# Storing the activated feed-forward input by groups of four tokens, 35 and 37 lines apart, ahead of the down projection

## The chip, the core and the metric

The kernel runs on one core of a Trainium2 chip. The metric is the device time of one execution in microseconds (us), the median of several runs; lower is better.

## What is computed

Two transformer-like blocks run on 256 tokens of width 1024. The change touches only the last layer of the second block, a gated feed-forward network:

```python
D_MODEL = 1024
D_FF = 3 * D_MODEL
...
def second_block(x, mem, ...):
    ...
        x = x + merged @ w_out[l]

        h2 = rms_norm(x, norm_ffn[l])
        up = causal_dwconv(h2 @ w_up[l], ffn_conv_w[l], ffn_conv_b[l])
        gate_h, val_h = jnp.split(up, 2, axis=-1)
        x = x + (jax.nn.gelu(gate_h, approximate=True) * val_h) @ w_down[l]
    return rms_norm(x, final_norm)
```

The product of the gelu and `val_h` is the activated feed-forward input: 3072 features by 256 tokens. The last matrix product multiplies it by `w_down` (3072 x 1024).

## The kernel before

All activations are held transposed: features on the 128 partitions, tokens along the free dimension. A matrix of 1024 features is 8 tiles (`KD`) of 128 x 256; the activated input has 24 (`KF`).

**Precision.** Every product is made from two parts of each operand, a rounded high part and the rest as a low part, and three products: high weight by high input, high weight by low input, low weight by high input. Weights are streamed from HBM in tiles of 128 x 1024 (512 KB). SP issues the transfers into `raw` (two chunks of two tiles, v = 0 and 1). ACT rounds a tile into `w_hi[v]` (L1378), POOL, in some stages DVE, writes `w_lo[v] = raw - w_hi` (L466). TensorE waits for `hi_ready[v]` and `lo_ready[v]`, and gives `w_hi[v]` and `w_lo[v]` free by `hi_used[v]` and `tile_done[v]`.

**Token order in a matmul.** In nearly all products the 256 tokens of the moving operand are not read in their order in memory. `spread` (L432) turns them into four rounds: a round takes every fourth group of four tokens (16 bytes), so that successive groups lie 64 bytes apart; the output in PSUM is written by the same pattern, so each token's result still lands in its own place.

```python
def spread(tile):

    return tile.rearrange("p (j g c) -> p g j c", g=4, c=4)
```

**Up stage** (about 1376 to 1498 us of the span). TensorE makes chunk n of the up projection (48 matmuls, L679 and L698). For each chunk DVE scales the result (L2612), ACT makes the last tap of the convolution (L1861, twice), DVE the others (L2624), ACT the gelu (L1867), DVE the product with `val_h` into a PSUM tile `ffp` (L2639); then ACT rounds it into plane n of `f_hi` (L1872) and DVE writes `f_lo = ffp - f_hi` (L2644). ACT also rounds the two weight tiles of the next chunk in between. Planes n lie one behind the other, each 256 tokens in their order: `f_hi` and `f_lo` are [128, 24, 256].

**Down stage** (1498 to 1564.5 us). 12 chunks: four pairs of output tiles (`pr`) by three thirds of the features (`g`). For each chunk and each of its two weight tiles (v) come three times 8 matmuls of 128 x 128 by 128 x 256: `w_hi` by `f_hi`, `w_hi` by `f_lo`, `w_lo` by `f_hi` (L1282), 576 in all. They accumulate in half a PSUM bank each. Nothing else is on TensorE in this stage. The order is written out by hand in program order on each engine.

**Tail** (from 1564.5 us). The last output tile is added to the residual, and the final norm is made and stored.

`f_hi` and `f_lo` lie inside the large SBUF region `big`, between `m_lo` and `x_hi`, `x_lo`. `yout`, the output ahead of its store, is carved from `big` behind `f_lo` (at `AT_X`, over `x_hi`).

Of the kernel before, what the change touches and what calls it, by code (L numbers as in the profile page):

```python
# [30 lines left out]
F32R = mybir.dt.float32r  # L31
# [3 lines left out]
ALU = mybir.AluOpType  # L35
ACT = mybir.ActivationFunctionType
AX = mybir.AxisListType

P = 128
T = 256  # L40
TT = T // P
D = 1024
KD = D // P
# [6 lines left out]
GROUP = 8  # L50
GATE_PARTS = 2
GATE_SCALE = 2.0 ** 14


CONV_W = 31
# [20 lines left out]
KF = DFF // P  # L76
# [90 lines left out]
def build(nc, t):  # L167
    plan, order = plan_chunks()
    ctx = ExitStack()
    with ctx:  # L170
        def sb(name, shape, dt=F32):
            return ctx.enter_context(nc.sbuf_tensor(name, shape, dt))
# [13 lines left out]
        w_hi = [sb(f"w_hi{v}", [P, TILE], F32R) for v in range(2)]  # L186
        w_lo = [sb(f"w_lo{v}", [P, TILE], F32R) for v in range(2)]
# [28 lines left out]

        y_hi = sb("y_hi", [P, KD, T], F32R)
        y_lo = sb("y_lo", [P, KD, T], F32R)
        m_lo = sb("m_lo", [P, KD, T], F32R)
        f_hi = sb("f_hi", [P, KF, T], F32R)  # L220
        f_lo = sb("f_lo", [P, KF, T], F32R)
        x_hi = sb("x_hi", [P, KD, T], F32R)
        x_lo = sb("x_lo", [P, KD, T], F32R)
        AT_M, AT_X, AFTER_X = (n * KD * T for n in (2, 9, 11))

        def carver(base, start=0):
            at = [start]

            def carve(*shape, rows=P, dt=F32):
                n = math.prod(shape) // (2 if dt in (BF16, F16) else 1)  # L230
                v = base[0:rows, at[0]:at[0] + n]
                at[0] += n
                assert at[0] <= base.shape[1], (at[0], shape)
                if dt != F32:
                    v = v.bitcast(dt)[:, 0:math.prod(shape)]
                names = "abcd"[:len(shape)]
                if len(shape) == 1:
                    return v
                return v.rearrange(f"p ({' '.join(names)}) -> p {' '.join(names)}",
                                   **dict(zip(names, shape)))  # L240
            return carve
# [4 lines left out]
        carve = carver(big)  # L246
# [15 lines left out]
        carve = carver(big, AFTER_X)  # L262
# [10 lines left out]
        carve = carver(big, 64 * T)  # L273
# [14 lines left out]
        carve = carver(small)  # L288
# [7 lines left out]
            "p b n (g i o) -> p b n g i o", g=GROUP // 2, o=2)  # L296
        hot2 = carve(2, GROUP // 2 * P * 2, dt=F16).rearrange("p b (g i o) -> p b g i o", g=GROUP // 2, o=2)

        a_hi, a_lo = [act_parts[:, i:i + 4, :].rearrange("p (c v) t -> p c v t", c=2) for i in (0, 4)]
        memT = small[:, 0:KD * T].rearrange("p (k t) -> p k t", t=T)  # L300

        carve = carver(big, KD * T)
# [27 lines left out]
        carve = carver(big, AT_M)  # L330
# [4 lines left out]
        carve = carver(big, AT_M + 5 * KD * T)  # L335
# [3 lines left out]
        carve = carver(big, AT_M + 2 * KD * T)  # L339
        spare = carve(2, KD, C96)  # L340

        carve = carver(big, 3 * KD * T)
# [10 lines left out]
        carve = carver(small)  # L353
# [7 lines left out]
        carve = carver(big, KD * T)  # L361
        uc = carve(2, 2, T)
        ffg, ffp = [[aux[n + b][:, 0:T] for b in range(2)] for n in (0, 2)]
        carve = carver(big, AT_X)
        yout = carve(KD, T)
        DOWN_TILES = ((0, 2), (2, 4), (4, 6), (6, 7), (7, 8))
        OUT_TILES = ((0, 2), (2, 4), (4, 6), (6, 8))
        carve = carver(big, KD * T + 4 * T)
# [6 lines left out]
        hi_ready = [sem(f"hi_ready{v}") for v in range(2)]  # L375
        lo_ready = [sem(f"lo_ready{v}") for v in range(2)]
# [55 lines left out]
        def spread(tile):  # L432

            return tile.rearrange("p (j g c) -> p g j c", g=4, c=4)
# [222 lines left out]
        def _(pe):  # L657
# [205 lines left out]
            for k in range(2):  # L863
                mm = pe.matmul(aux[2][:, 0:T], ones[:, :], sq[:, k, :], start=(k == 0), stop=(k == 1))
# [42 lines left out]
            for k in range(KD // 2):  # L907
                mm = pe.matmul(aux[3][:, 0:T], ones[:, :], sq[:, k, :], start=(k == 0), stop=(k == KD // 2 - 1))
# [3 lines left out]
            for j in range(HEADS + 1):  # L912
                if j and j + 1 < HEADS:
                    scores(j + 1)
                if j:
                    turn_probs(j - 1)
                    name, i, v = beside_heads[j - 1]
# [20 lines left out]
            for g in range(TT * 4):  # L938
# [5 lines left out]
                for i in range(4):  # L944
                    v, at = divmod(h0 + i, HALVES // 2)
                    mm = pe.matmul(aux[g % 4][:, i * NK:(i + 1) * NK], qp[:, h0 + i, tt * P:(tt + 1) * P],  # L946
                                   raw[kc.raw][v][:, at * NK:(at + 1) * NK], start=True, stop=True)
# [14 lines left out]
            for n, src in enumerate((e1, e2, sc)):  # L962
                for tt in range(TT):
                    mm = pe.transpose(aux[n][:, tt * P:(tt + 1) * P],
                                      src[:, tt].rearrange("p h k -> p (h k)"), ident[:, :])
# [126 lines left out]
            for h in range(GH):  # L1092
                mm = pe.matmul(pair(aux[h // 2], GDK)[:, h % 2, :], wdec[:, h, :], dec, start=True, stop=True)
# [5 lines left out]
            for h in range(K96):  # L1099
                if h in MQ_TILES:  # L1100
                    n = MQ_TILES.index(h)
# [56 lines left out]
            for tt in range(TT):  # L1158
                for h in range(GH):
                    mm = pe.transpose(aux[tt][:, h * GDK:(h + 1) * GDK], ekd[:, h, tt * P:(tt + 1) * P],  # L1160
                                      ident[0:GDK, 0:GDK])
# [4 lines left out]
            for h in range(GH):  # L1166
                for n in range(NCH):
                    lo, cols = (n % 2) * GCHUNK, slice(n * GCHUNK, (n + 1) * GCHUNK)
                    at_col = (h * TT + n // 2) * GCHUNK
                    mm = pe.matmul(aux[2][lo:lo + GCHUNK, at_col:at_col + GCHUNK], emg[:, h, cols],  # L1170
                                   eg[:, h, cols], start=True, stop=True)
# [99 lines left out]
            for i, c in enumerate(plan["down"]):  # L1271
                pr, g = divmod(i, 3)
                if i == 0:
                    pe.wait_ge(ffn_act, KF - 1)
                pe.wait_ge(ffn_split, KD * (g + 1) if pr == 0 else KF)
                for v in range(2):
                    out = gemm[1][:, 0:T] if pr == 3 and v else pair(aux[pr])[:, v, :]
                    for w, x, ready in ((w_hi, f_hi, hi_ready), (w_hi, f_lo, hi_ready), (w_lo, f_hi, lo_ready)):
                        pe.wait_ge(ready[v], c.split + 1)
                        for k in range(KD):  # L1280

                            mm = pe.matmul(spread(out), w[v][:, k * P:(k + 1) * P], spread(x[:, g * KD + k, :]),  # L1282
                                           start=(g == k == 0 and (v == 0 or pr == 3) and w is w_hi and x is f_hi),
                                           stop=(g == 2 and w is w_lo and k == KD - 1), skip_group_check=True)
                        if x is f_lo:
                            mm.then_inc(hi_used[v], 1)
                    mm.then_inc(tile_done[v], 1)
                if pr == 1 and g == 1:
                    moved(pe, plan["up"])
# [18 lines left out]
        def _(act):  # L1308
# [560 lines left out]
            def ffn_round(b, n):  # L1869
                act.wait_ge(ffn_act, n + 1)  # L1870
                plane = slice(n, n + 1) if isinstance(n, int) else bass.ds(n, 1)
                act.activation(f_hi[:, plane, :].rearrange("p a t -> p (a t)"), ffp[b],  # L1872
                               ACT.Copy).then_inc(ffn_rounded, 1)

            def up_step(s, n, it=0, first=False):
                c = plan["up"][s]
# [35 lines left out]
        def _(dve):  # L1912
# [728 lines left out]
            def ffn_subtract(b, n):  # L2641
                dve.wait_ge(ffn_rounded, n + 1)
                plane = slice(n, n + 1) if isinstance(n, int) else bass.ds(n, 1)
                dve.tensor_tensor(f_lo[:, plane, :].rearrange("p a t -> p (a t)"), ffp[b],  # L2644
                                  f_hi[:, plane, :].rearrange("p a t -> p (a t)"),
                                  ALU.subtract).then_inc(ffn_split, 1)

            def ffn_step(s, n, it=0, first=False):
                if not first:
# [129 lines left out]
```

## Time and profile before

| what | value |
|---|---|
| median of 3 runs | 1576.95 us (1575.48 to 1577.13) |
| the profiled execution | 1575.39 us |
| its span, first to last instruction | 1573.3 us |
| TensorE busy in the span | 99% |
| mean granted clock of TensorE | 0.999 of 2.4 GHz |

The page gives each engine's busy time, and the chain of work that ended last, which is followed back from the last instruction. Matmuls overlap, one starting while the one before still drains, so that a single matmul's duration says little. What counts is the time from one matmul's start to the next: a piece of the chain, divided by its number of matmuls.

### The profile page before, as it was taken

How to read it: one execution, taken by the hardware profiler on the slowest of the kernel's cores; microseconds unless marked ns; L12 is line 12 of the kernel's file. 1: busy time of each engine (PE TensorE's matmuls, PEld its weight loads, DVE VectorE, ACT ScalarE, POOL GpSimd, SP SyncE). 2: the span in 40 equal slices, each digit the busy share in tenths (PEclk: the TensorE clock that was granted, in tenths of full speed). 3: DMA queues.
4: the chain of work that ended last, by engine and by line, in shares of the span. 5: the costliest groups of instructions: out<-in, count | busy, mean ns of one | idle time of the engine just before them, and what ended most of it. 6: DMA issues, size and time to landing. Idle time of an engine off the chain costs nothing.

```text
span 1573.3 us, 33476 instructions
## 1 busy us (share of the span) xinstructions
PE 1559.8 (99%) x12568; PEld 1471.2 (94%) x12568; DVE 1070.1 (68%) x1867; ACT 880.9 (56%) x1251; POOL 883.9 (56%) x413
## 2 busy tenths in 40 slices
PE   9999999999999999999999999999999999999998
PEld 8999899999999999998888888889999999999998
DVE  7998743879933777778888766676937484455522
ACT  6566765554454444444444445557677654676653
POOL 8786468968886000000000244457876689898886
PEclk9999999999999999999999999999999999999999
DMA  6564335555555555555555665556543356565553
GB/s 223 171 197 157 107 123 188 192 183 190 191 183 196 176 163 183 173 167 170 185 177 170 218 195 193 196 200 189 173 143 107 118 170 190 192 199 188 189 196 124
DMA packets 86217, 277.03 MB, mean 176 GB/s; under 512 B 11232, under 2 KB 18160, under 8 KB 86128
## 3 DMA queue, kind: packets, MB, share of 16 engines
q1 hardware_dynamic: 85712, 274.76, 53.7%
q8 instruction: 59, 0.97, 0.2%
q0 software_dynamic: 272, 1.05, 0.2%
q14 instruction: 30, 0.25, 0.1%
q10 hardware_dynamic: 144, 0.00, 0.0%
HBM read 274.73 MB, written 1.05 MB: 175 GB/s over the span
## 4 chain that ended last, share of the span: by engine, by line
PE 92%; issue 2%; DVE 2%; POOL 2%; ACT 2%; DMA 0%; SPq 0%; DVEq 0%; ACTq 0%; POOLq 0%
PE gemm L679 35%; PE gemm L996 22%; PE gemm L698 18%; PE aux L1282 4%; PE gemm L827 3%; PE aux L976 2%; POOL w_lo L466 1%; PE gemm L714 1%; PE gemm L739 1%; ACT w_hi L1378 1%; PE gemm L1282 1%; PE aux L946 0%; PE gemm L813 0%; PE gemm L720 0%; PE gemm L756 0%
## 5 line engine op out<-in xcount | busy, mean ns | idle before, releaser
L466 POOL TENSOR_TENSOR w_lo<-raw,w_hi 128x1024 fp32r<-128x1024 f32 (+1 forms) x330 | 789.8, 2402 | 279.9 <-ACT w_hi L1378 275.8
L1378 ACT ACTIVATE w_hi<-raw 128x1024 fp32r<-128x1024 f32 (+1 forms) x492 | 514.7, 1048 | 556.8 <-PE gemm L679 310.4
L679 PE MATMUL gemm<-h_lo,w_hi 128*128 128x256 f32 x2144 | 504.7, 277 | 0.0
L679 PE MATMUL gemm<-h_hi,w_hi 128*128 128x256 f32 x2096 | 499.8, 279 | 1.1 <-ACT w_hi L1378 1.0
L679 PEld LDWEIGHTS gemm<-h_lo,w_hi 128*128 128x128 f32 x2144 | 402.8, 188 | 0.7 <-issue 0.2
L679 PEld LDWEIGHTS gemm<-h_hi,w_hi 128*128 128x128 f32 x2096 | 394.3, 188 | 3.8 <-issue 1.6
L698 PE MATMUL gemm<-h_hi,w_lo 128*128 128x256 f32 x2096 | 284.6, 277 | 2.4 <-POOL w_lo L466 1.5
L698 PEld LDWEIGHTS gemm<-h_hi,w_lo 128*128 128x128 f32 x2096 | 259.8, 188 | 4.9 <-POOL w_lo L466 3.4
L466 DVE TENSOR_TENSOR w_lo<-raw,w_hi 128x1024 fp32r<-128x1024 f32 x162 | 195.5, 1221 | 100.6 <-ACT w_hi L1378 99.5
L996 PE MATMUL gemm<-w_hi,act_parts 128*128 128x512 f32 x1008 | 247.9, 386 | 0.4 <-ACT act_parts L1579 0.4
L996 PEld LDWEIGHTS gemm<-w_hi,act_parts 128*128 128x128 f32 x1008 | 187.6, 187 | 36.6 <-issue 0.5
L627 POOL DMA_DIRECT2D small<-in_memT x1 | 1.0, 1027 | 379.2 <-DVE big L2315 379.2
L996 PE MATMUL gemm<-w_lo,act_parts 128*128 128x512 f32 x504 | 133.5, 385 | 0.0
L2321 DVE TENSOR_TENSOR act_parts<-big,act_parts 128x512 fp32r<-128x512 f32 x64 | 89.5, 1398 | 45.9 <-ACT act_parts L1579 45.8
L996 PEld LDWEIGHTS gemm<-w_lo,act_parts 128*128 128x128 f32 x504 | 94.3, 187 | 18.9 <-DVE w_lo L466 0.3
L2058 DVE SCALAR_TENSOR_TENSOR aux<-big,params,aux 128x256 f32<-128x256 f32 x240 | 94.7, 489 | 0.0
L462 POOL TENSOR_TENSOR w_lo<-raw,w_hi 128x768 fp32r<-128x768 f32 x30 | 59.0, 1968 | 17.8 <-ACT w_hi L1375 17.0
L679 PE MATMUL gemm<-f_hi,w_hi 128*128 128x256 f32 x256 | 60.5, 276 | 0.0
L2307 DVE TENSOR_TENSOR small<-small 128x512 f16<-128x512 f16 x128 | 57.1, 488 | 0.0
L2624 DVE SCALAR_TENSOR_TENSOR big<-gemm,params,big 128x255 f32<-128x255 f32 (+1 forms) x96 | 39.7, 476 | 24.6 <-ACT big L1861 24.6
L679 PEld LDWEIGHTS gemm<-f_hi,w_hi 128*128 128x128 f32 x256 | 48.1, 188 | 0.1
L2304 DVE TENSOR_TENSOR small<-small 128x1024 f16<-128x1024 f16 x64 | 43.8, 685 | 0.0
(436 smaller groups left out, 2175.9 us busy)
## 6 DMA issues: line engine op xcount, KB each, us to landing
raw<-in_w_u SPq DMA_DIRECT2D x128, 512.0 KB, 3.5
raw<-in_w_ev SPq DMA_DIRECT2D x128, 512.0 KB, 3.6
raw<-in_w_up SPq DMA_DIRECT2D x48, 512.0 KB, 3.5
raw<-in_w_gate SPq DMA_DIRECT2D x24, 512.0 KB, 3.8
raw<-in_w_down SPq DMA_DIRECT2D x24, 512.0 KB, 3.5
raw<-in_w_conv_in SPq DMA_DIRECT2D x16, 512.0 KB, 4.3
raw<-in_w_peer_q SPq DMA_DIRECT2D x16, 512.0 KB, 3.8
raw<-in_w_branch SPq DMA_DIRECT2D x24, 288.0 KB, 2.8
```

The costliest lines, as they stand in the source:

```text
L462: eng.tensor_tensor(lo[:, :, 0:C96], by_k(raw[c.raw][v], C96), hi[:, :, 0:C96], ALU.subtract)
L466: eng.tensor_tensor(w_lo[v][:, 0:n], raw[c.raw][v][:, 0:n], w_hi[v][:, 0:n], ALU.subtract).then_inc(lo_ready[v], 1)
L679: return pe.matmul(spread(out), w[:, k, :], spread(x[n][:, k, :]), start=(n == k == 0), stop=False)
L698: mm = pe.matmul(spread(out), w[:, k, :], spread(x[0][:, k, :]), start=False, stop=(k == steps - 1))
L827: mm = pe.matmul(spread(pair(gemm[c.bank])[:, tt, :]), x[:, v * KD // 2 + k, tt * P:(tt + 1) * P], spread(w[:, k, :]), start=(begins and t ...
L996: mm = pe.matmul(spread(gemm[2 * half + tt][:, :]), a[:, c.raw, v, tt * P:(tt + 1) * P], spread(w[v][:, half * (D // 2):(half + 1) * (D // ...
L1282: mm = pe.matmul(spread(out), w[v][:, k * P:(k + 1) * P], spread(x[:, g * KD + k, :]), start=(g == k == 0 and (v == 0 or pr == 3) and w is ...
L1378: act.activation(w_hi[v][:, 0:n], raw[c.raw][v][:, 0:n], ACT.Copy).then_inc(hi_ready[v], 1)
L2058: ins = dve.scalar_tensor_tensor(acc, zc[:, k, w:w + T], tap, acc, ALU.mult, ALU.add)
L2304: dve.tensor_tensor(hot2[:, b], each(iota2, P), along(e2T[:, tokens], P), ALU.is_equal)
L2307: ins = dve.tensor_tensor(hot1[:, b, part], hot[:, b], along(gate_parts[:, part, tokens], P // 2), ALU.mult)
L2321: dve.tensor_tensor(a_lo[:, c.raw, :, :], act_peer[:, plane, :], a_hi[:, c.raw, :, :], ALU.subtract).then_inc(a_split, 1)
```

## The change

The two parts of the activated input go into two new tensors, `f_groups_hi` [128, 64, 35, 4] and `f_groups_lo` [128, 64, 37, 4]: for each group of four tokens 35 (37) lines of 16 bytes, of which the first 24 hold the 24 planes. Successive groups of tokens of one plane so lie 560 (592) bytes apart. The tensors cover the same addresses as `m_lo`, `f_hi`, `f_lo`, `x_hi` and `x_lo` together (64 x 72 lines is 9 times 8 x 256 values), and `yout` moves behind them.

ACT's rounding and DVE's subtraction write (and DVE reads) 64 pieces of 16 bytes in place of one run of 1024 bytes. The matmuls of the down stage with v = 0 read the 64 groups in their order, in one round, and write PSUM contiguously. Those with v = 1 read the even groups and then the odd ones, in two rounds, with PSUM written the same way. Number, order and waits of the instructions are the same on every engine. All other products keep `spread`, and where `f_hi` and `f_lo` serve earlier stages they stay.

```diff
+F_PITCH = (35, 37)
...
+        with (nc.sbuf_tensor("f_groups_hi", [P, T // 4, F_PITCH[0], 4], F32R) as f_groups_hi,
+              nc.sbuf_tensor("f_groups_lo", [P, T // 4, F_PITCH[1], 4], F32R) as f_groups_lo):
+            pass
         m_lo = sb("m_lo", [P, KD, T], F32R)
         f_hi = sb("f_hi", [P, KF, T], F32R)
         f_lo = sb("f_lo", [P, KF, T], F32R)
...
+        f_parts = [g[:, :, :, :].rearrange("p g k c -> p k g c")[:, 0:KF] for g in (f_groups_hi, f_groups_lo)]
...
-        carve = carver(big, AT_X)
+        carve = carver(big, 2 * KD * T + sum(F_PITCH) * T)
         yout = carve(KD, T)
...
                     out = gemm[1][:, 0:T] if pr == 3 and v else pair(aux[pr])[:, v, :]
-                    for w, x, ready in ((w_hi, f_hi, hi_ready), (w_hi, f_lo, hi_ready), (w_lo, f_hi, lo_ready)):
+                    rounds = v + 1
+                    out = out.rearrange("p (j g c) -> p g j c", g=rounds, c=4)
+                    for w, n, ready in ((w_hi, 0, hi_ready), (w_hi, 1, hi_ready), (w_lo, 0, lo_ready)):
                         pe.wait_ge(ready[v], c.split + 1)
                         for k in range(KD):
 
-                            mm = pe.matmul(spread(out), w[v][:, k * P:(k + 1) * P], spread(x[:, g * KD + k, :]),
-                                           start=(g == k == 0 and (v == 0 or pr == 3) and w is w_hi and x is f_hi),
+                            mm = pe.matmul(out, w[v][:, k * P:(k + 1) * P],
+                                           f_parts[n][:, g * KD + k].rearrange("p (j g) c -> p g j c", g=rounds),
+                                           start=(g == k == 0 and (v == 0 or pr == 3) and w is w_hi and n == 0),
...
-                act.activation(f_hi[:, plane, :].rearrange("p a t -> p (a t)"), ffp[b],
-                               ACT.Copy).then_inc(ffn_rounded, 1)
+                act.activation(f_parts[0][:, plane].rearrange("p a g c -> p (a g) c"),
+                               ffp[b].rearrange("p (g c) -> p g c", c=4), ACT.Copy).then_inc(ffn_rounded, 1)
...
-                dve.tensor_tensor(f_lo[:, plane, :].rearrange("p a t -> p (a t)"), ffp[b],
-                                  f_hi[:, plane, :].rearrange("p a t -> p (a t)"),
-                                  ALU.subtract).then_inc(ffn_split, 1)
+                dve.tensor_tensor(f_parts[1][:, plane].rearrange("p a g c -> p (a g) c"),
+                                  ffp[b].rearrange("p (g c) -> p g c", c=4),
+                                  f_parts[0][:, plane].rearrange("p a g c -> p (a g) c"), ALU.subtract).then_inc(ffn_split, 1)
```

## Rows read from the trace of the kernel before

**Rows 1.** The page, busy time by engine: us, share, instructions.

```profile
PE 1559.8 (99%) x12568; PEld 1471.2 (94%) x12568; DVE 1070.1 (68%) x1867; ACT 880.9 (56%) x1251; POOL 883.9 (56%) x413
```

**Rows 2.** The chain that ended last, from 1498 us: start, us, engine, line, instructions.

```profile
1498.66 52.11 PE aux L1282 x456
1550.78 2.75 PE gemm L1282 x24
1553.52 2.74 PE aux L1282 x24
...
1561.75 2.76 PE gemm L1282 x24
1564.51 0.02 issue
1564.53 0.43 DVE xres L2676
```

**Rows 3.** Windows, 1500 to 1560 us: busy us (instructions), granted clock, DMA share, GB/s.

```profile
1500.00:1560.00 60.00, 60.00 (x528) 60.00 (x527) 10.10 (x14) 30.05 (x37) 52.31 (x23) 1.00 0.53 175
```

**Rows 4.** The chain, 234 to 252 us, the same kind of matmul on `x_hi` and `x_lo`.

```profile
236.78 1.87 PE gemm L679 x16
238.64 0.93 PE gemm L698 x8
...
249.84 0.93 PE gemm L698 x8
250.78 1.23 PE gemm L714 x9
```

**Rows 5.** The chain, 699 to 720 us, matmuls of 512 columns on `act_parts`.

```profile
699.79 9.29 PE gemm L996 x41
```

**Rows 6.** Timeline of TensorE: bf16 of 512 columns, fp32 of 256 columns in two passes.

```profile
1565.92 0.81 PE L804 MATMUL aux<-zeros 128*128 128x512 bf16 x3
1175.85 1.03 PE L1118 MATMUL aux<-big 96*128 96x256 f32 x4
```

**Rows 7.** Instructions of L804, L1118: durations ns min/median/max, first and last start.

```profile
L804 PE MATMUL aux<-zeros x5: 376/377/377, 1564.7 to 1566.3; 128*128 128x512 bf16 x5
L1118 PE MATMUL aux<-big x32: 377/378/382, 1175.8 to 1207.2; 96*128 96x256 f32 x32
```

**Rows 8.** Timeline of ACT in one chunk of the up stage.

```profile
1487.77 0.37 ACT L1872 ACTIVATE f_hi<-aux 128x256 f32 x1
1488.62 1.02 ACT L1861 ACTIVATE big<-gemm,params 128x256 f32<-128x256 f32 x2 [0.48 <-DVE gemm L2612]
1489.53 1.05 ACT L1378 ACTIVATE w_hi<-raw 128x1024 fp32r<-128x1024 f32 x1
```

**Rows 9.** Timeline of DVE in the same chunk.

```profile
1487.68 0.70 DVE L2612 TENSOR_TENSOR gemm<-gemm,rstd 128x512 f32<-128x512 f32 x1 [1.10 <-PE gemm L698]
1488.30 0.42 DVE L2644 TENSOR_TENSOR f_lo<-aux,f_hi 128x256 f32 x1
1489.80 1.65 DVE L2624 SCALAR_TENSOR_TENSOR big<-gemm,params,big 128x255 f32<-128x255 f32 x4 [1.08 <-ACT big L1861]
```

**Rows 10.** Timelines of the down stage: ACT, then POOL.

```profile
1522.52 1.06 ACT L1378 ACTIVATE w_hi<-raw 128x1024 fp32r<-128x1024 f32 x1 [1.67 <-PE aux L1282]
...
1520.92 2.38 POOL L466 TENSOR_TENSOR w_lo<-raw,w_hi 128x1024 fp32r<-128x1024 f32 x1 [0.19 <-ACT w_hi L1378]
1523.65 2.39 POOL L466 TENSOR_TENSOR w_lo<-raw,w_hi 128x1024 fp32r<-128x1024 f32 x1 [0.36 <-ACT w_hi L1378]
```

**Rows 11.** The two instructions that write the parts: durations ns min/median/max.

```profile
L1872 ACT ACTIVATE f_hi<-aux x24: 363/367/384, 1379.0 to 1503.1; 128x256 f32 x20, 128x256 fp32r<-128x256 f32 x4
L2644 DVE TENSOR_TENSOR f_lo<-aux,f_hi x24: 414/425/426, 1379.4 to 1503.5; 128x256 f32 x20, 128x256 fp32r<-128x256 f32 x4
```

More of the change, by code:

```diff
@@ L1277, in _ @@
                     out = gemm[1][:, 0:T] if pr == 3 and v else pair(aux[pr])[:, v, :]
-                    for w, x, ready in ((w_hi, f_hi, hi_ready), (w_hi, f_lo, hi_ready), (w_lo, f_hi, lo_ready)):
+                    rounds = v + 1
+                    out = out.rearrange("p (j g c) -> p g j c", g=rounds, c=4)
+                    for w, n, ready in ((w_hi, 0, hi_ready), (w_hi, 1, hi_ready), (w_lo, 0, lo_ready)):
                         pe.wait_ge(ready[v], c.split + 1)
                         for k in range(KD):
-                            mm = pe.matmul(spread(out), w[v][:, k * P:(k + 1) * P], spread(x[:, g * KD + k, :]),
-                                           start=(g == k == 0 and (v == 0 or pr == 3) and w is w_hi and x is f_hi),
+                            mm = pe.matmul(out, w[v][:, k * P:(k + 1) * P],
+                                           f_parts[n][:, g * KD + k].rearrange("p (j g) c -> p g j c", g=rounds),
+                                           start=(g == k == 0 and (v == 0 or pr == 3) and w is w_hi and n == 0),
                                            stop=(g == 2 and w is w_lo and k == KD - 1), skip_group_check=True)
-                        if x is f_lo:
+                        if n == 1:
                             mm.then_inc(hi_used[v], 1)
```

## The prediction

> **What bounds the kernel now.** I read the page's busy times first. TensorE is busy 99% of the span, the next engine 68% [rows 1]. That only says where to look, since matmuls overlap. The chain that ended last says more: from 1498.66 us it lies on L1282 alone, 576 matmuls without a gap, until 1564.51 us, when the tail begins with DVE's addition [rows 2]. The whole down stage is thus the pace of one kind of matmul. That pace is 52.11 us / 456 = 114.3 ns in the first piece, and (1564.51 - 1498.66) / 576 = 114.3 ns over the whole. The windows have 528 of them in 60.00 us, which agrees, and show that the granted clock is 1.00 of 2.4 GHz [rows 3]. At 2.4 GHz, 256 columns take 106.7 ns in the array. So 7.6 ns of each matmul, 4.4 us in the stage, is not array time. That is all that a change of the access pattern alone could ever give here, 0.28% of the run.
>
> The other resources of the stage have room. ACT rounds a weight tile in 1.06 us and then idles 1.67 us until TensorE gives the next one free. POOL needs 2.39 us per tile and waits 0.36 us, at the shortest 0.19 us, for ACT [rows 10]. A tile lasts TensorE 24 x 114.3 = 2.74 us. POOL could keep up with 2.39 + 0.19 = 2.58 us, which is 107.5 ns per matmul. The transfers bring 175 GB/s with the DMA engines 53% busy [rows 3].
>
> **The change part by part.**
>
> *No instruction is added, removed or moved*, and no wait changes. What changes is how long three kinds of instruction take.
>
> *ACT's rounding and DVE's subtraction* (24 each) now write 64 pieces of 16 bytes. Before they take 0.367 and 0.425 us [rows 11]. No row shows an ACT or DVE instruction of this size with such pieces, so I bound it: at the least nothing, at the most twice the time, +0.37 and +0.43 us. ACT's next instruction behind the rounding, the last tap, waits 0.48 us for DVE's scaling, which ended at 1488.38 us [rows 8, 9]. So a rounding that ends up to 0.48 us later moves nothing on ACT. Behind it is queued the rounding of the next weight tile (1489.53 us), and only a loss beyond the 0.48 us would reach that, and through POOL TensorE. DVE idles 1.08 us behind the subtraction until ACT's taps are there [rows 9]; +0.37 us of later start and +0.43 us of longer work, 0.80 us, still fit. The last rounding ends at about 1503.5 us [rows 11]. Its plane is first read in the third chunk of the down stage, 96 matmuls or 11 us after 1498.66, at 1509.6 us. **I cost both at nothing.**
>
> *The 576 matmuls* are the only term on the path. Two things change in each: where the moving operand's groups of 16 bytes lie (64 bytes apart before, 560, 592 or double that after), and the order in which PSUM is written. No row shows such a pattern, so it is bounded by the nearest ones:
> - Below: what a matmul costs when its operand's pattern is no burden. Three bf16 matmuls of 512 columns take 0.81 us together, of which the last one's duration is 0.377 us [rows 6, 7]: (0.81 - 0.377) / 2 = 216.5 ns each, 3.2 ns above the 213.3 ns of array time. Four two-pass fp32 matmuls, also 512 array columns each, give (1.03 - 0.378) / 3 = 217.3 ns, 4.0 ns above [rows 6, 7]. Rounding makes both uncertain by some 4 ns. With 3.2 ns above, a 256-column matmul would take 109.9 ns: 576 x (109.9 - 114.3) = **-2.5 us**. The array time itself, 106.7 ns, is the hard end: -4.4 us.
> - Above: the same instruction form with the same `spread`, on `x_hi` and `x_lo`, runs at (250.78 - 236.78) us / 120 = 116.7 ns [rows 4]. Where the operands lie is thus worth 2.4 ns here. The same loss in the down stage would be 576 x 2.4 = **+1.4 us**.
>
> How does the 7.6 ns grow with the columns? The 512-column matmuls of the same pattern take 9.29 us / 41 = 226.6 ns [rows 5], or 221.2 ns if one record is missing there, 8 to 13 ns above array time. So a good part of the excess grows with the columns read and is not a fixed price per instruction. That is the part an access pattern can touch. But rows 6 leave only 3 to 4 ns as fixed, and every pattern before and after still jumps once per 16 bytes. I see no reason in the rows why a longer jump should remove the whole of it, and one (rows 4) that addresses matter at all. I take half of the way to 109.9 ns: 112.1 ns, 576 x -2.2 = **-1.3 us**, with -0.4 and -2.2 us as the ends of this case.
>
> Is the stage blind to the read side? Rows 4 show it isn't: there every group has 16 bytes in one piece as here, and the pace differs by 2.4 ns. The Trainium skill, page "SBUF — State Buffer", section "Specifications (TRN2)", has SBUF in 16-byte cachelines that give full bandwidth from two hits per line on. Both patterns read four fp32 of a line, so by this rule the read side costs the same before and after, whatever the pitch, and the sum would be 0 us. The trace does not agree that this is the whole story. The Trainium skill's page "TensorE: Matmul & The Clock Gate", section "Back-to-back issue gap", gives 262 cycles for 256 columns, 109.2 ns; taken as the floor the sum would be 576 x -5.1 = -2.9 us. The trace has no 256-column matmul as fast as that.
>
> *The tail* is as before: `yout` is only elsewhere. 0 us.
>
> **Sum.** Against the profiled execution (span 1573.3 us, 1575.39 us in all): 1575.4 - 1.3 = 1574.1 us. That execution was 1.6 us under the median of the three runs, 1576.95 us. The prediction is of a median: 1576.95 - 1.3 = **1575.7 us**.
>
> **The rivals.**
>
> 1. *The pattern costs what it did.* The excess is that of high-rate fp32 streaming, or of the weight load beside it, and neither cares where the groups lie. For it: on TensorE's timeline every product with `spread` has nearly the same pace, 114.3 ns here. Against it: rows 4. It gives 1577.0 us, give or take 0.4.
>
> 2. *The floor.* Groups at odd distances never collide with anything, and a matmul takes 109.9 ns or less. For it: rows 6 show TensorE streaming with 3 to 4 ns of excess. Against it: those rows read half the bytes per ns. It gives 1576.95 - 2.5 = 1574.4 us; the array time alone 1572.5 us.
>
> 3. *Only the v = 0 half gains,* because its output is now contiguous in PSUM while v = 1 still writes in jumps. 288 matmuls go to 109.9 ns: 288 x -4.4 ns = -1.3 us, 1575.7 us. In time it can't be told from the forecast; the pace of the two halves tells. The Trainium skill's page "PSUM — Partial Sum Buffer", section "Specifications (TRN2)", says that any non-contiguous pattern there slows matmuls significantly. The trace limits "significantly" to the 7.6 ns, since the patterns of rows 2 do jump in PSUM. I count this with the forecast.
>
> 4. *Slower: the longer jumps stall the read.* The place is the stream of the moving operand in the down stage. If a fourth of the 64 groups lost one array cycle (0.417 ns), a matmul would take 6.7 ns more, 121.0 ns: +3.8 us, 1580.8 us. If every second one did, +7.7 us. It decides from 3.15 us / 576 = 5.5 ns per matmul, 13 lost cycles in 64 groups. For it: the pitch changes from 4 lines to 35, 37, 70 and 74, and nothing in the trace has run such a stride at this rate; the present pattern is likely to have been better than plain order for some reason of this kind. Against it: rows 4, the worst of its form, is only 2.4 ns away.
>    The small form of this rival is the +1.4 us of rows 4: 1578.4 us.
>
> 5. *ACT's writes overrun the 0.48 us.* That needs a rounding of over 0.85 us, more than twice as long as now. Then 21 chunks of the up stage would each lose the rest, 0.1 us more per chunk being 2 us. I give it 2 in 100.
>
> **How the numbers follow.** A measurement of this kernel tells about 0.2%, 3.15 us, from no change: faster means under 1573.8, slower over 1580.1 us. Chances: forecast with rival 3, 0.41 (1574.7 to 1576.6 us); rival 1, 0.25; rival 2, 0.12; the small loss of rows 4, 0.11; rival 4, 0.09; rival 5, 0.02. Only the part of rival 2 beyond 3.15 us, and the scatter of the runs (1575.48 to 1577.13 us), make faster: 0.07. Slower is rival 4 and rival 5, less where they fall short: 0.10. Same: 0.83. The range leaves out some 0.1 on each side: 1573.6 to 1580.0 us. It holds the bounds -2.5 and +1.4 us and stops short of -4.4 us and of rival 4.
>
> **What the profile of the changed kernel would show.** The chain of the down stage, divided by 576: 112 ns is the forecast, 114.3 rival 1, under 110 rival 2, over 120 rival 4. The starts of the matmuls by v, 24 at a time: equal paces speak for the read side, a fast v = 0 beside a slow v = 1 for PSUM or for the number of rounds. High and low parts apart (8 at a time) tell the pitches 35 and 37. The durations of the rounding and the subtraction, and ACT's idle time ahead of the last tap (0.48 us less what they lengthen), test the cost of nothing; the pace of the up stage must stay. The down stage must still start at once behind the up stage, and POOL's wait for ACT must stay above zero. **What would make the prediction wrong:** a pace outside 109.9 to 116.7 ns, or an up stage that got longer.

## The result and the profile after

| | median us | runs |
|---|---|---|
| before | 1577.18 (1575.48 to 1578.19) | 6 |
| changed | 1588.02 (1587.09 to 1588.54) | 6 |

The ratio is 1.0069, with a 95% interval of 1.0059 to 1.0080: the change makes the kernel 10.8 us **slower**. The prediction had 1575.7 us, a range of 1573.6 to 1580.0, and 0.10 on slower.

The chain of the changed kernel, the lines that answer to [rows 2] (start us, us, engine, line, instructions; L1289 is the down projection's matmul there):

```profile
1496.41 1.84 PE gemm L684 x16
1498.25 0.92 PE gemm L703 x8
1499.16 60.69 PE aux L1289 x456
1559.86 3.49 PE gemm L1289 x24
1563.34 2.95 PE aux L1289 x24
...
1572.70 3.49 PE gemm L1289 x24
1576.19 0.02 issue
```

The up stage is what it was: 1.84 and 0.92 us per tile. The down stage begins 0.5 us later and lasts 1576.19 - 1499.16 = 77.03 us in place of 65.85. The two profiled executions are 1587.09 - 1575.39 = 11.7 us apart: these 11.2 us, and the 0.5 us ahead of the stage, which lie within the scatter of the runs. TensorE still never waits in the stage. Its matmuls are farther apart, 133.7 ns in the mean. In the last chunks the chain shows the two weight tiles one by one: v = 0 takes 2.95 us (`aux`), v = 1 takes 3.49 us (`gemm`), where before both took 2.74.

TensorE's timeline of one chunk in the middle shows the parts, 8 matmuls each (start us, us, then what). A group's length is seven distances and one matmul's own duration, so the column to compare is the second:

```profile
1531.08 1.11 PE L1289 MATMUL aux<-f_groups_hi,w_hi 128*128 128x256 f32 x8
1532.03 1.23 PE L1289 MATMUL aux<-f_groups_lo,w_hi 128*128 128x256 f32 x8
1533.09 1.10 PE L1289 MATMUL aux<-f_groups_hi,w_lo 128*128 128x256 f32 x8
1534.03 1.40 PE L1289 MATMUL aux<-f_groups_hi,w_hi 128*128 128x256 f32 x8
1535.25 1.19 PE L1289 MATMUL aux<-f_groups_lo,w_hi 128*128 128x256 f32 x8
1536.27 1.40 PE L1289 MATMUL aux<-f_groups_hi,w_lo 128*128 128x256 f32 x8
```

In v = 0 (first three lines) the low part, 37 lines apart, is the slow one. In v = 1 the two rounds double the distances, and now the high part, 70 lines apart, is slow and the low part, 74 lines apart, the quicker one. From the matmuls' starts in a steady stretch the paces are: 35 lines 116 to 118 ns, 37 lines 133.7 ns, 70 lines in two rounds 153.7 ns, 74 lines in two rounds 127 ns. Neither the part nor the weight tile alone orders these. The distance read might.

The writes cost nothing, as the timeline of ACT shows in the up stage; the answer to [rows 8]:

```profile
1488.27 0.37 ACT L1880 ACTIVATE f_groups_hi<-aux 128x256 f32 x1
1489.12 1.02 ACT L1869 ACTIVATE big<-gemm,params 128x256 f32<-128x256 f32 x2 [0.48 <-DVE gemm L2620]
1490.03 1.06 ACT L1386 ACTIVATE w_hi<-raw 128x1024 fp32r<-128x1024 f32 x1
```

The rounding still takes 0.37 us and the idle time ahead of the last tap is still 0.48 us. Of all 24, the durations are those of [rows 11]:

```profile
L1880 ACT ACTIVATE f_groups_hi<-aux x24: 365/366/384, 1379.4 to 1503.6; 128x256 f32 x20, 128x256 fp32r<-128x256 f32 x4
L2652 DVE TENSOR_TENSOR f_groups_lo<-aux,f_groups_hi x24: 414/425/426, 1379.8 to 1504.0; 128x256 f32 x20, 128x256 fp32r<-128x256 f32 x4
```

### The profile page after: what moved, and what is told of

It reads as the page before. It is cut to its first block, busy times and chain, and to the rows that moved or that the text cites. A ratio compares the mean times of both kernels' runs of the same rounds, so it can differ in the third digit from the quotient of the medians.

```text
span 1585.0 us, 33476 instructions
## 1 busy us (share of the span) xinstructions
PE 1570.4 (99%) x12568; PEld 1482.6 (94%) x12568; DVE 1067.9 (67%) x1867; ACT 881.0 (56%) x1251; POOL 883.4 (56%) x413
## 4 chain that ended last, share of the span: by engine, by line
PE 92%; issue 2%; DVE 2%; POOL 2%; ACT 2%; DMA 0%; SPq 0%; DVEq 0%; ACTq 0%; POOLq 0%
PE gemm L684 35%; PE gemm L1001 22%; PE gemm L703 18%; PE aux L1289 4%; PE gemm L832 3%; PE aux L981 2%; POOL w_lo L471 1%; PE gemm L719 1%; PE gemm L744 1%; PE gemm L1289 1%; ACT w_hi L1386 1%; PE aux L951 0%; PE gemm L818 0%; PE gemm L725 0%; PE gemm L761 0%
```

## The experiments

Paces below are the mean distance from one matmul's start to the next within a tile of 24, from the third matmul on. Chain pieces are shown for those on which a verdict rests.

### One round for both weight tiles

```diff
-                    rounds = v + 1
+                    rounds = 1
```

> The changed kernel, but both weight tiles (v = 0 and 1) read the 64 groups in one round. Theory A (the distance between groups read one after the other sets the pace: 35 lines 117 to 118 ns, 37 lines 133 ns, 70 lines 153 ns, 74 lines 128 ns): the v = 1 half falls to the v = 0 half's pace, all 24 tiles take 2.94 us, the down stage 70.6 us in place of 77.0, the kernel some 6.5 us less than the changed one, about 1581.5 us. Rival B (the second weight tile's place, or its half of the PSUM bank, is what is slow): v = 1 stays at 145 ns, no change against the changed kernel.

Median 1581.29 us beside 1576.73 us for the kernel before on the same chip, ratio 1.0028 (1.0018 to 1.0037). The chain:

```profile
1500.11 55.88 PE aux L1289 x456
1555.99 2.93 PE gemm L1289 x24
1558.92 2.93 PE aux L1289 x24
```

Here `gemm` is v = 1, and it is as quick as `aux`, v = 0. The stage lasts 70.6 us (1500.11 to 1570.70). Theory A gave 70.6 us and 1581.5 us. The second weight tile and its half of the PSUM bank are innocent (rival B falls). The two rounds cost 6.4 of the 11.2 us. They doubled the distance and changed the order of the PSUM writes at once; the next experiment and the one on PSUM order and weights tell the two apart.

### The order of the PSUM writes alone

```diff
-                            mm = pe.matmul(spread(out), w[v][:, k * P:(k + 1) * P], spread(x[:, g * KD + k, :]),
+                            mm = pe.matmul(out.rearrange("p (g j c) -> p g j c", g=4, c=4), w[v][:, k * P:(k + 1) * P], spread(x[:, g * KD + k, :]),
```

> The kernel before, with its storage and its reads in four rounds, but the down projection's results written to PSUM in plain order (so its outputs have the tokens of the down projection permuted). Theory A (reads alone set the pace): 114.3 ns per matmul as before, no change. Rival (the order of writing PSUM matters): another pace; a gain of up to 7.6 ns per matmul, 4.4 us, if jumps in PSUM were what costs the 7.6 ns.

```profile
1500.28 52.13 PE aux L1282 x456
1552.41 2.73 PE gemm L1282 x24
```

52.13 us for 456 matmuls, against 52.11 in [rows 2]: 114.3 ns. With these reads, the order in which PSUM is written changes nothing, so the 7.6 ns over the array time are not paid there, and rival 3 of the prediction falls with them. The Trainium skill, page "PSUM — Partial Sum Buffer", section "Specifications (TRN2)", says that any non-contiguous pattern in PSUM slows matmuls significantly. This measurement does not agree for jumps every 16 bytes.

### Sweep of the distance

The matmuls of the second to the twelfth chunk read one tensor at 22 distances, one for each tile:

```diff
+                    s = STRIDES[2 * i + v]
...
+                                read = bass.AP(read.tensor, read.offset, [list(read.ap[0]), [4 * s, T // 4], [1, 4]])
+                            mm = pe.matmul(out.rearrange("p (j c) -> p j c", c=4), w[v][:, k * P:(k + 1) * P], read,
```

> The changed kernel with the down projection's reads replaced: from the second chunk on each tile of 24 matmuls reads 64 groups of 16 bytes at one distance, 1 line in the first tile of the second chunk, then 2, 3, up to 22 lines in the last; all write PSUM in plain order (the outputs are not the reference's, and a fill of the region ahead of the up stage costs time there). Theory A1 (only the distance modulo a small power of two matters, since the lines lie in interleaved banks): the pace repeats, 3 lines like 35 (117 ns), 5 like 37 (133 ns), 6 like 70 (153 ns), 10 like 74 (128 ns), and 4 gives 114 ns. Theory A2 (a long distance as such is slow): paces rise slowly with the distance, all under 117 ns up to 22 lines, or jump at a certain distance.

> The second sweep: distances of 35 to 44, 48, 64 to 72, 24 and 23 lines, one for each tile of 24 matmuls from the second chunk on (outputs are not the reference's, as in the first sweep). Modulo 16: 35 gives 117.0 ns (3), 36 119.6, 37 134.1, 38 160.8, 39 120.8, 40 125.2, 41 118.4, 42 126.6, 43 119.6, 44 119.5, 48 and 64 144.7 (16), 65 117.6, 66 118.0, 67 117.0, 68 119.6, 69 134.1, 70 160.8, 71 120.8, 72 125.2, 24 125.2, 23 120.8. If another modulus than 16 holds, 39 to 44 and 24 miss these by over 3 ns.

Chain pieces of the first sweep, one window each, for 4, 5, 6 and 16 lines (24 matmuls are 23 distances and a little more, so the pieces are compared with one another):

```profile
1527.15 2.86 PE aux L1292 x24
...
1530.01 3.20 PE aux L1292 x24
...
1533.20 3.81 PE aux L1292 x24
...
1563.56 3.42 PE aux L1292 x24
```

And of the second sweep, for 37 and 38 lines:

```profile
1524.03 3.19 PE aux L1292 x24
...
1527.22 3.81 PE aux L1292 x24
```

5 and 37 lines take 3.20 and 3.19 us, 6 and 38 lines both 3.81. All 44 distances, in ns for one matmul, by what is left when the distance is divided by 16 lines (256 bytes):

| left of 16 | distance in lines: ns |
|---|---|
| 1 | 1: 117.6, 17: 117.9, 65: 118.0 |
| 2 | 2: 118.0, 18: 118.0, 66: 117.5 |
| 3 | 3: 117.0, 19: 117.0, **35: 117.2**, 67: 117.0 |
| 4 | 4: 119.6, 20: 119.6, 36: 120.1, 68: 119.5 |
| 5 | 5: 134.1, 21: 134.1, **37: 134.0**, 69: 134.0 |
| 6 | 6, 22, 38: 160.8, **70: 160.7** |
| 7 | 7: 120.8, 23, 39, 71: 120.9 |
| 8 | 8: 125.2, 24: 125.0, 40, 72: 125.2 |
| 9 | 9: 118.4, 41: 118.3 |
| 10 | 10: 126.6, 42: 126.5 (**74** would be here) |
| 11 | 11: 119.6, 43: 119.5 |
| 12 | 12: 119.5, 44: 119.5 |
| 13, 14, 15 | 13: 134.5, 14: 119.4, 15: 118.4 |
| 0 | 16: 144.7, 48: 144.3, 64: 144.1 |

The first sweep set the table, and the second came out within 0.6 ns of what the remainder foretold. Length does not matter: 3 lines cost what 67 cost. The remainder modulo 256 bytes does, from 117.0 to 160.8 ns. So the period of theory A1 is there and theory A2 falls. That the lines lie in banks, which A1 gives as the reason, no run shows. Two of A1's figures missed: 4 lines take 119.6 and not 114 ns, and 6 lines 160.8 and not 153. The four distances of the change have the remainders 3, 5, 6 and 10, that is one good one and three of the bad ones. In the changed kernel the two-round reads take 153.7 and 127 ns beside 160.7 and 126.6 here. They have one jump back in the middle, a sweep tile has none; whether that is worth the 7 ns at 70 lines was not tried.

### PSUM order and weights held against the distance

```diff
+                    s, r, m, wide = STRIDES[2 * i + v]
...
+                            left = w[v][:, k * P:k * P + m]
+                            if wide > 1:
+                                left = w[v][:, k:k + 127 * wide + 1:wide]
```

> As the sweep, but tiles with chosen distance, rounds, width of the weight tile and spacing of the weights' columns. Distance 4 lines in 1, 2, 4 and 8 rounds of both read and PSUM pattern; 35 and 70 lines in 1, 2 and 4 rounds (2 rounds double the distance). Then weight tiles of 64 and 32 columns beside distances of 4, 35, 37 and 70 lines, then weight columns 32 bytes apart beside the same distances. Theory C (the moving read collides with the weight load beside it): with 32 weight columns in place of 128 the excess over 106.7 ns falls to about a fourth, so 70 lines give some 118 ns in place of 153; with weight columns that touch a new line each, all paces rise. Theory A alone (the moving read collides with itself): 70 lines stay at 153 ns with narrow weight tiles, and the weights' spacing changes nothing at 4 lines.

Other than the expectation says, the number of rounds changed the order of the PSUM writes only in this kernel; the reads kept their distance. Tiles with fewer weight columns leave out the rest of the output.

| distance | PSUM in 1, 2, 4, 8 rounds | 64, 32 weight columns |
|---|---|---|
| 4 | 120.2, 119.7, 119.8, 119.3 | 119.7, 121.0 |
| 35 | 117.0, 117.0, 118.0 | 115.3, 114.8 |
| 37 | | 134.0, 134.0 |
| 70 | 161.0, 160.7, 160.7 | 160.8, 160.7 |

70 lines with 32 weight columns, in the chain (22 matmuls stand in this piece: 3.54 us / 22 = 160.9 ns):

```profile
1572.57 3.54 PE gemm L1297 x22
```

The output's order is worth 1 ns at most at any of these distances. The number of weight columns changes nothing at the bad distances, though the weight load gets shorter with them (198 to 119 ns at 70 lines), where theory C wanted some 118 ns. So theory C, that the collision with the weight load makes the bad distances slow, falls. Why the load itself takes longer at bad distances (188 to 199 ns) is not shown.

The last four tiles took the 128 weight columns 32 bytes apart. Here theory A missed: it had no change at 4 lines, and all four paces rose, as theory C said. But they rose to one value. That is another limit: a weight load of 338 to 341 ns, and a matmul every 241.8, 242.4, 241.4 and 245.2 ns for 4, 35, 37 and 70 lines, so nearly whatever the distance. The chain piece for 4 lines:

```profile
1576.43 5.51 PE aux L1297 x23
```

### Fewer partitions, and what the clock showed by chance

The same distances on the first 96, 64 and 32 partitions (the others' products are left out):

```diff
+                                read = flat[0:s[1], 4 * k:4 * k + 252 * s[0] + 4]
...
+                                left = left[0:s[1]]
```

> As the first sweep (outputs are not the reference's), but from the second chunk on the matmuls use only the first 96, then 64, then 32 partitions of both operands, each with distances of 3, 4, 5, 6, 10, 13 and 16 lines, and in the last tile 6 lines with all 128. Theory D1 (the collision is within one partition's own memory, line against line): nothing changes with fewer partitions, 117, 119.6, 134, 160.8, 126.6, 134.5, 144.7 ns each time. Rival D2 (partitions that share memory are read at different moments as the operand passes down the array, and collide with each other): with 32 partitions the slow distances 5, 6, 13 and 16 come down toward 117 ns.

| partitions | 3 | 4 | 5 | 6 | 10 | 13 | 16 lines |
|---|---|---|---|---|---|---|---|
| 96 | 116.8 | 120.7 | 134.1 | 160.8 | 126.5 | 134.1 | 144.4 |
| 64 | 117.0 | 120.4 | 134.1 | 160.8 | | | |

So down to 64 partitions the cost does not depend on their number. It is not a total of all partitions that has a limit. After some matmuls on 64 of the 128 rows, in the tile with 10 lines, the granted clock fell from 1.00 to 0.50 (1.2 GHz), which it had not done in the tiles on 96 rows, and stayed there nearly to the end. Two windows, with the columns of [rows 3]:

```profile
1530.00:1550.00 20.00, 20.00 (x151) 19.82 (x150) 2.08 (x2) 7.79 (x9) 14.79 (x7) 1.00 0.52 162
1585.00:1605.00 20.00, 20.00 (x96) 20.00 (x96) 0.00 (x0) 3.78 (x4) 9.46 (x4) 0.50 0.06 23
```

At that clock all seven distances, with 32 partitions, took the same 213.3 ns, which is 256 columns at 1.2 GHz and nothing beside it. The chain for 6 lines, at full clock on 64 partitions and at half clock on 32:

```profile
1551.25 3.81 PE aux L1295 x24
...
1586.17 4.91 PE gemm L1295 x23
```

Thus the tiles on 32 partitions tell nothing of the distances at full clock, and rival D2 stays open for groups of fewer than 64 partitions. But the half clock tells something better. The distances of 10, 13 and 16 lines on 64 partitions ran at half clock too, at 213.3 ns from the second of them on. The last tile, 6 lines on 128 partitions, began at 213.3 ns and ended at 160.6 ns, when the clock had come back. So the worst distance costs nothing as long as the array takes its columns slowly. If a piece of 16 bytes needs 160.8 / 64 = 2.5 ns at 6 lines whatever the array's clock, it fits into the 213.3 / 64 = 3.3 ns that it has at half clock; that is an estimate.

The end of that last tile settles one more rival, which no expectation names: a collision of the read with the other engines or the transfers. There no other engine and no transfer is at work (behind the two numbers of TensorE come DVE, ACT and POOL, all at 0, and the DMA share is 0), and the 6 lines still take 160.6 ns:

```profile
1610.30:1611.60 1.30, 1.30 (x11) 1.30 (x10) 0.00 (x0) 0.00 (x0) 0.00 (x0) 1.00 0.00 0
```

### A remainder of 1 for both parts

If the remainder is the cause, the changed kernel should be cured by two other numbers, with everything else left as it is. 33 and 66 lines have the remainders 1 and 2:

```diff
-F_PITCH = (35, 37)
+F_PITCH = (33, 33)
```

> The changed kernel with one number altered: both parts at 33 lines in place of 35 and 37; v = 0 in one round, v = 1 in two, as changed. If the distance modulo 16 lines sets the pace, 33 lines are like 1 (117.6 ns) and the two rounds' 66 lines like 2 (118.0 ns): every tile takes 2.83 us, the down stage 67.8 us against 65.85 us before and 77.0 us as changed, so about 1578.9 us. If two rounds as such, the grouped storage or distances of over 22 lines are slow, v = 1 stays above 125 ns and the kernel above 1582 us.

Median 1578.37 us beside 1576.12 us, ratio 1.0014 (1.0005 to 1.0024).

```profile
1501.12 53.77 PE aux L1289 x456
1554.89 2.85 PE gemm L1289 x24
1557.74 2.82 PE aux L1289 x24
```

The stage lasts 67.95 us, 118.0 ns per matmul, and 117.5 to 118.8 in the single tiles. The changed kernel had 77.03 us. So 9.1 of the 11.2 us hang on the numbers 35 and 37, and 2.1 us remain with 33 lines, read in the same one and two rounds.

### Why the pattern of before is better than any single distance

A constant 4 lines takes 119.6 ns, but the kernel before, also 4 lines apart and with jumps back, takes 114.3 [rows 2]. First the order of before with other numbers of rounds, and other pieces:

```diff
+                        rounds, run = STRIDES[at]
+                        return tile.rearrange("p (j g c) -> p g j c", g=rounds, c=run)
```

> The kernel before, its storage and its results unchanged; only the order in which the down projection's matmuls read a plane of 256 tokens (and write it to PSUM) differs from tile to tile: rounds x tokens in a piece (4,4) as before, then (1,4), (2,4), (8,4), (16,4), (32,4), (64,4), (4,4), (2,8), (4,8), (8,8), (16,8), (2,16), (4,16), (8,16), (2,2), (4,2), (8,2), (16,2), (32,2), (2,32), (4,32), (1,4), (4,4). By the first sweep, where r rounds of 16-byte pieces are a distance of r lines: plain order 117.6 ns, 2 rounds 118.0, 4 rounds 114.3 as before (and not 119.6: the jump back after 16 pieces is then worth 5 ns), 8 rounds 125, 16 rounds 145, 32 rounds 145 unless the jumps back help there too. Pieces of 8 or 16 tokens lie between plain order and these. Pieces of 2 tokens (half a line at a time) are slower than all, above 150 ns. A pattern under 113 ns would be one that beats the kernel before.

In ns by (rounds, tokens of a piece): (4, 4) 114.3 and 114.8, in the last tile 116.9; (1, 4), which is plain order, 118.2; (2, 4) 117.8; (8, 4) 123.4; (16, 4) 135.7; (32, 4) 127.3; (64, 4), plain order again, 118.3. Pieces of 8, 16 or 32 tokens take 115.0 to 122.5. Pieces of two tokens take 217.9 to 233.2. The four rounds of before are the best of these, 3.9 ns better than plain order. The expectation was too high for 16 and 32 rounds, 145 ns, where the distance alone was reckoned with.

The two-token pieces bear on the page that the prediction weighed. The Trainium skill, "SBUF — State Buffer", section "Specifications (TRN2)", gives full bandwidth from two hits per 16-byte line on. The same row has a penalty for each cross to a new line, without a size. For this fp32 stream the runs disagree with the first: two in a row of a line take 218 to 233 ns. Nor does counting the crosses help: with four in a row there are 64 pieces in every pattern, and they take anything from 113 to 161 ns.

Then the seam between rounds, free of the kernel's layout. A pattern is (distance in lines, pieces in a round, lines from one round's start to the next, lines from one matmul's start to the next):

```diff
+                                s1, n1, s2, step = s
+                                read = bass.AP(read.tensor, read.offset + 4 * step * k,
+                                               [list(read.ap[0]), [4 * s2, T // 4 // n1], [4 * s1, n1], [1, 4]])
```

> A third sweep (outputs are not the reference's): patterns with a jump after a run of groups. In each tile: distance within the run, groups in the run, distance from run to run, shift from matmul to matmul, in lines: (4,16,1,64), (4,16,1,1), (4,16,64,64), (4,16,65,64), (4,16,66,64), (4,16,67,64), (4,16,72,64), (4,8,33,64), (4,4,17,64), (4,32,129,64), (1,16,16,64), (1,16,17,64), (1,16,18,64), (1,16,20,64), (1,8,9,64), (1,4,5,64), (3,16,48,64), (3,16,49,64), (3,16,50,64), (2,16,33,64), (2,32,65,64), (9,16,145,1). Theory: the pace depends on remainders modulo 16 alone, the jump's as well. Then the first is the kernel before's pattern, 114.3 ns; (4,16,65,64) is the same modulo 16 and also 114.3; (4,16,64,64) has no jump and gives 119.6; the second, with another shift from matmul to matmul, stays within 1 ns of the first if the seam between two matmuls does not matter. If it is the turning back as such that helps, (4,16,65,64) gives 119.6. Any pattern under 113 ns would be worth building in.

The chain for (4, 16, 1, 64), which is the kernel before, for (4, 16, 64, 64), whose rounds have no seam, and for (4, 16, 65, 64), the same with one line more at each seam:

```profile
1517.59 2.77 PE aux L1297 x24
...
1523.14 2.86 PE aux L1297 x24
...
1526.00 2.76 PE aux L1297 x24
```

That is 114.5, 120.1 and 114.3 ns. The jump back over 59 lines is not what helps; the shift by one line is, three times in a matmul. A shift of 2 lines (66) gives 114.0, 3 lines (67) 116.5, 8 lines (72) 119.9. With the distance 1, seams help by 1 ns at most (116.6 to 122.2 ns), and with 2 not at all (117.8 and 120.0). The best is a distance of 3 with a shift by one line, (3, 16, 49, 64): 113.3 ns. And the shift from one matmul to the next matters too: (4, 16, 1, 1), one line, takes 115.9 where 64 lines take 114.5, which is 0.4 ns more than the expectation allowed.

> A fourth sweep (outputs are not the reference's), the tiles' patterns as (distance in the run, groups in the run, distance of the runs, shift from matmul to matmul) in lines: (3,16,49,1), (3,16,49,2), (3,16,49,16), (3,16,47,64), (3,16,51,64), (3,16,53,64), (3,8,25,64), (3,32,97,64), (3,4,13,64), (4,16,69,64), (4,16,71,64), (4,16,74,64), (4,16,78,64), (12,16,193,1), (11,16,177,1), (14,16,225,1), (9,16,146,1), (15,16,241,1), (17,16,273,1), (1,16,19,64), (7,16,113,1), (1,32,34,64). Theory: all of distances 1, 3, 4, 9, 11, 12, 14, 15, 17 lie between 113 and 120 ns whatever the jumps, the shift of the first three is worth under 2 ns, and nothing comes below 112 ns, since some 5 to 6 ns over the array's 106.7 ns are not the pattern's. Rival: a well chosen jump gets below 111 ns.

(3, 16, 47, 64) takes 113.3 ns as well. (3, 16, 49) with 1, 2 and 16 lines between matmuls takes 115.8, 114.7 and 114.3. So this shift is worth up to 2.5 ns here. The others lie from 114.2 to 120.9 ns. Of some 100 patterns measured, none is under 113.3 ns, and the rival (below 111 ns) falls.

### Two kernels with a seam

Both keep the new storage, and take from the last sweeps what fits it. The first reads pitch 33 in four rounds, so its distance is 132 lines (remainder 4) and its seam is one line off:

```diff
-                    rounds = v + 1
+                    rounds = 4
```

> The changed kernel with both parts at 33 lines and every matmul of the down projection in four rounds. Modulo 16 its distances (132 lines) are like 4, and its jumps back (from 60 x 33 to 33 lines, like 5) are like those of the kernel before. If the remainders modulo 16 decide everything, the pace is that of before, 114.3 ns: down stage 65.8 us, the kernel at 1576 to 1577 us, a ratio of 1.000 to before, the grouped storage and its 64-piece writes costing nothing. If the storage itself or far distances cost, it stays at 117 ns or more, 1.5 us over before.

The second stores both parts 35 lines apart in four runs of 16 pieces, with one line more between runs:

```diff
+        RUN = 16 * F_PITCH + 1
+        with (nc.sbuf_tensor("f_groups_hi", [P, 4, RUN, 4], F32R) as f_groups_hi,
+              nc.sbuf_tensor("f_groups_lo", [P, 4, RUN, 4], F32R) as f_groups_lo):
```

> The changed kernel with both parts at 35 lines (3 modulo 16), one empty line more after each 16 groups, and every matmul of the down projection reading in one round of four runs: the pattern (3,16,49) of the third sweep modulo 16, which ran at 113.3 ns with a shift of 64 lines from matmul to matmul. Here the shift is 1 line; the third sweep's pair (4,16,1) with 64 and with 1 line differed by 1.5 ns. So 113.3 to 115 ns: down stage 65.3 to 66.2 us, within 0.6 us of the kernel before, ratio 1.000. If a remainder of 3 in the pitch is not what makes the pace, it is at 117 ns or above, 1.6 us over before.

| | median us | beside it before | ratio | stage us | ns |
|---|---|---|---|---|---|
| pitch 33, four rounds | 1579.49 | 1578.19 | 1.0007 (0.9998 to 1.0016) | 66.75 | 115.9 |
| runs of 16, pitch 35 | 1578.97 | 1577.35 | 1.0008 (0.9999 to 1.0017) | 67.0 | 116.1 |

The first piece of each chain, against 52.11 us in [rows 2]:

```profile
1502.91 52.83 PE aux L1289 x456
```

```profile
1501.12 53.04 PE aux L1289 x456
```

Both missed their expectations, on the slow side. The first had 114.3 ns, for remainders that decide everything, and took 115.9. That is (4, 16, 1, 1) of the sweep to 0.1 ns: here too a matmul starts one line after the last one, which the expectation left out. The second was over its 113.3 to 115 ns by 1 ns, and (3, 16, 49, 1) at 115.8 shows why: consecutive matmuls start one line apart in this storage, not 64. Neither beats the kernel before, in whose layout consecutive matmuls start 64 lines apart anyway. The best pattern found, 113.3 ns, would gain 576 x 1.0 ns = 0.6 us, which no comparison here could tell.

## Why the prediction was wrong

**The bound was right.** The down stage is the pace of one kind of matmul, before and after, and the whole of the loss stands in the chain on that line.

**The terms at nothing were right.** The rounding takes 365/366/384 ns and the subtraction 414/425/426 ns, with 64 pieces as with one run. The 0.48 us of idle time stayed, the up stage's pace stayed, and the tail is as before.

**The pace was wrong**, -2.2 ns forecast and +19.4 ns come (133.7 - 114.3), far outside the 109.9 to 116.7 ns that the prediction named itself. The term that failed is that of the 576 matmuls: -1.3 us in the sum, +11.2 us in the runs. Two steps of its working failed:

- *The upper bound of +2.4 ns from [rows 4].* It took the difference between `x_hi` and the activated input for what addresses can be worth. But the rows of this kind of matmul, [rows 2] and [rows 4], both read by `spread`, at distances of 4 lines with the same seams. Rows that share one pattern bound no other. The range for an unseen pattern had to be wide on that side: the worst distance is 160.8 - 114.3 = 46.5 ns, 27 us over 576 matmuls.
- *Half of the way to 109.9 ns.* No row stood behind the gain. [rows 6] read at half the bytes per ns, as the text itself said against rival 2. The excess is there in every pattern tried in the down stage at full clock and is never under 113.3 - 106.7 = 6.6 ns in the mean of a tile. The kernel before, 1.0 ns above the least, had nearly nothing left to gain.

The rivals, one by one. Rival 1 (no change) falls with the result. Rival 2 (the floor) is not reached by any pattern. Rival 3 (PSUM) falls: contiguous writes alone give 114.3 ns. Rival 4 is what came, at a chance of 0.09: the longer jumps stall the read of the moving operand. Its place was right. Its size was not, 121.0 ns against 133.7 (and +7.7 us in its larger form against +11.2), and its picture was not: it is not the length of the jump that stalls but what is left of it modulo 256 bytes. Rival 5 (ACT's writes) falls.

The 11.2 us are made up so, from one tile's first start to the next one's: the twelve tiles of v = 0 take 2.95 in place of 2.74 us, 12 x 0.21 = 2.5 us, most of it the low part's 37 lines. The twelve of v = 1 take 3.47, 12 x 0.73 = 8.7 us. In each of these tiles 16 matmuls read the high part at 153.7 ns and 8 the low part at 127 ns, which is 16 x 39.4 = 0.63 us and 8 x 12.7 = 0.10 us over 114.3, so most of it is the high part's 70 lines.

What stays open: why 5, 6, 10, 13 and 0 are the slow remainders, and why the table is not symmetric (6 gives 160.8 ns, 10 gives 126.6, though each is the other read backward). The cause is thus shown as far as the distance modulo 256 bytes; what in the memory or its port makes it so is open. Where the last 6.6 ns at the best patterns are spent was not found, nor why [rows 4] is 2.4 ns slower than [rows 2]; the shift from matmul to matmul, worth 1.4 to 2.5 ns in the sweeps, was not tried on it.

## What to carry to other kernels

Ahead of changing the stride of a TensorE moving operand like this one (fp32, 256 columns), divide the distance between its 16-byte pieces by 256 bytes and look up what is left in the table: an odd number of lines protects from nothing, 37 is as bad as 5. A trace whose rows all share one access pattern can't bound another one; one kernel that gives each tile its own pattern settles 22 of them in a single run. Where TensorE waits for nothing and still is slower than its columns, vary the read of the moving operand before the output or the weights.

## What the runs showed of the hardware

- The pace of fp32 matmuls of 256 columns depends on the distance of the moving operand's 16-byte pieces with a period of 256 bytes: 117.0 ns (3 lines) to 160.8 ns (6 lines).
- It does not depend on the order of the PSUM writes (within 1 ns), nor, at the bad distances, on 128, 64 or 32 weight columns, nor on 128, 96 or 64 partitions (64 with 3, 4, 5 and 6 lines). At 6 lines it is the same with all other engines and the transfers at rest, 160.6 ns.
- It is gone at a granted clock of 0.50: 213.3 ns for seven distances on 32 partitions, and for 6 lines on 128.
- Pieces of 8 bytes take 218 to 233 ns. Weight columns 32 bytes apart take 241 to 245 ns, with the weight load at 338 to 341 ns.
- At distances of 3 and 4 lines, patterns that shift by one line three times in a matmul are better than a constant distance: 114.5 against 120.1 ns with 4 lines, 113.3 against 115.3 with 3, both with 64 lines from matmul to matmul.
- ACT and DVE write 64 pieces of 16 bytes in the time of one run of 256 elements: 366 and 425 ns.
